# Banded attention: the next pair's query projection by group 3, eight parts of the pair beyond at the border; the dilated branch's log counts in seven steps

## What is computed

```python
def token_mixer(x, w_in, b_forget, sinks, w_branch, w_gate, b_gate, w_out):
    (aq, ak, av, bq, bk, bv, cq, ck, cv, ciq, cik, ciw, dq, dk, dv, df) = jnp.split(x @ w_in, offsets, axis=-1)
    o_a, _, _ = banded_attention(heads(aq, A_HEADS), heads(ak, A_KV_HEADS), heads(av, A_KV_HEADS),
                                 slopes_a, A_WINDOW - 1, 1, sinks)          # window 128, 8 heads on 2 kv heads
    o_b = dilated_attention(heads(bq, B_HEADS), heads(bk, B_HEADS), heads(bv, B_HEADS), slopes_b)
    o_c = dsa_attention(...)
    o_d = forgetting_attention(...)
    proj = jnp.einsum('bsnk,nkd->bsnd', branches, w_branch)
    gates = jax.nn.sigmoid(x @ w_gate + b_gate)
    return jnp.sum(gates * proj, axis=2) @ w_out
```

## Time and profile before

| | us |
|---|---|
| median of 3 runs | 2135.15 (2134.28 to 2136.54) |
| profiled execution, its time | 2136.81 |
| profiled execution, its span | 2135.0 |
| PE busy | 2073.9 |
| DVE busy | 1558.0 |
| ScalarE (ACT) busy | 973.4 |
| GpSimd (POOL) busy | 934.7 |
| mean granted clock of TensorE | 0.991 |

### The profile page before, as it was taken

One profiled execution on the slowest core, in us unless ns is written; L12 is line 12 of the kernel. 1 busy time (PEld: TensorE's weight loads), 2 busy tenths in 40 slices (PEclk: granted clock), 3 DMA queues, 4 the chain that ended last, 5 costly groups with the idle time before them and its releaser, 6 DMA issues.

```text
span 2135.0 us, 28861 instructions
## 1 busy us (share of the span) xinstructions
PE 2073.9 (97%) x10350; PEld 1729.5 (81%) x10350; DVE 1558.0 (73%) x2596; ACT 973.4 (46%) x1752; POOL 934.7 (44%) x732
## 2 busy tenths in 40 slices
PE   8799999999999999999999999999999999999998
PEld 6578887888887888888887888878788888888887
DVE  5669888767687666698775766667877777775668
ACT  4443333655633565615743665432433333334541
POOL 5367762333322332322332333534765555555751
PEclk9999999999999999999999999999999999999999
DMA  4123332110042111041031000341566565558862
GB/s 129 41 86 117 104 111 78 21 31 27 14 148 60 50 41 38 22 167 30 21 105 44 11 21 21 119 157 49 159 188 202 182 196 172 158 196 306 276 208 94
DMA packets 197374, 224.27 MB, mean 105 GB/s; under 512 B 25704, under 2 KB 149608, under 8 KB 197232
## 3 DMA queue, kind: packets, MB, share of 16 engines
q1 hardware_dynamic: 194320, 212.43, 31.8%
q10 hardware_dynamic: 2912, 10.00, 1.3%
HBM read 164.17 MB, written 58.23 MB: 104 GB/s over the span
## 4 chain that ended last, share of the span: by engine, by line
PE 80%; DVE 11%; ACT 3%; issue 3%; POOL 2%; DMA 1%; ACTq 0%; DVEq 0%
PE pair L1315 13%; PE pair L894 13%; PE pair L1181 7%; PE obank L1315 5%; PE pair L878 5%; PE pair L1344 5%; PE obank L988 4%; PE chunk L967 4%; PE pair L939 3%; PE chunk L1344 3%; PE obank L1181 3%; PE pair L1274 3%; PE pair L940 3%; PE obank L1344 2%; DVE o_top L2327 2%
## 5 line engine op out<-in xcount | busy, mean ns | idle before, releaser
L2116 POOL TENSOR_TENSOR w_lo<-w_raw,w_hi 128x1024 fp32r<-128x1024 f32 x64 | 158.6, 2479 | 320.7 <-ACT w_hi L1608 320.5
L2517 DVE TENSOR_TENSOR pt_lo<-chunk,pt_hi 128x512 fp32r<-128x512 f32 (+1 forms) x272 | 173.7, 639 | 86.3 <-ACT pt_hi L1631 82.5
L1631 ACT ACTIVATE pt_hi<-chunk 128x512 fp32r<-128x512 f32 (+1 forms) x272 | 150.8, 555 | 171.3 <-PE chunk L967 169.9
L2164 POOL TENSOR_SCALAR prob<-prob,att 128x256 f32<-128x256 f32 (+4 forms) x172 | 117.9, 696 | 237.6 <-DVE att L2453 237.6
L894 PE MATMUL pair<-act_hi,w_hi 128*128 128x512 f32 x432 | 187.5, 434 | 1.1 <-DVE heads L2458 0.9
L894 PE MATMUL pair<-act_hi,w_lo 128*128 128x512 f32 x432 | 170.8, 395 | 0.0
L894 PE MATMUL pair<-act_lo,w_hi 128*128 128x512 f32 x432 | 170.2, 394 | 0.0
L2327 DVE TENSOR_SCALAR_CACHE_REDUCE o_top<-score,stat 128x384 uint8<-128x384 f32 (+1 forms) x186 | 166.6, 941 | 0.4
L988 PE MATMUL obank<-pt_hi,heads 128*128 128x256 f32 (+1 forms) x568 | 148.8, 286 | 1.9 <-DVE o_t L2525 1.2
L1727 ACT ACTIVATE prob<-prob,att 128x256 f32<-128x256 f32 (+4 forms) x172 | 120.5, 701 | 47.7 <-DVE att L2441 46.2
L988 PE MATMUL obank<-pt_lo,heads 128*128 128x256 f32 (+1 forms) x568 | 139.2, 281 | 0.0
(11 more groups left out here) (492 smaller groups left out, 5963.1 us busy)
## 6 DMA issues: line engine op xcount, KB each, us to landing
down_sums<-dn_sums SPq DMA_DIRECT2D x40, 512.0 KB, 6.3
w_raw<-in_w_in SPq DMA_DIRECT2D x37, 512.0 KB, 3.8
gates<-o_t SPq DMA_DIRECT2D x22, 512.0 KB, 2.9
up_raw<-in_w_up SPq DMA_DIRECT2D x22, 512.0 KB, 4.8
gate_raw<-in_w_ffn_gate SPq DMA_DIRECT2D x22, 512.0 KB, 6.0
hidden<-gelu_s SPq DMA_DIRECT2D x22, 512.0 KB, 3.4
dn_raw<-down_sums SPq DMA_DIRECT2D x44, 256.0 KB, 3.8
h_in<-down_sums SPq DMA_DIRECT2D x44, 256.0 KB, 4.7
```

Of the source, the lines that this page charges most:

```text
L2116: nc.gpsimd.tensor_tensor(split_into(1, g), w_raw[:, g % 2, 0:kt * cols], split_into(0, g).bitcast(F32), ALU.subtract).then_inc(lo_ready, 1)
L2517: nc.vector.tensor_tensor(pt_lo[:, n % PT_SLOTS, 0:m], t[:, 0:m], pt_hi[:, n % PT_SLOTS, 0:m].bitcast(F32), ALU.subtract).then_inc(chunk_f ...
```

## The change

`BESIDE[A]` puts all parts for the next pair in groups 0 to 3 (before: up to group 6) and eight of the pair beyond in groups 7 to 9 (before: four in groups 8 and 9); `AHEAD[A]` goes from 4 to 8, so eight parts stand before pair 0's loop, now run through `beside_v`'s branch of the loop, `fill(4)` and `fill(4)`. `BESIDE_LAST[A]` is unchanged, its first eight of sixteen places now count for its own turn. In pair 0, 1 and 2 the copy "q0" h 0 stands after group 2 instead of 3. `ln_counts` counts in seven steps instead of thirteen (a floor of the distance as integer, the low bits shifted into a float, compared with zero and added in one step); the five steps of the logarithm and the two biases stay. Five steps instead of eleven run before B's query copies.

```diff
--- before.py
+++ after.py
@@ -191,8 +191,8 @@
               (10, 2), (11, 1), (11, 1), (12, 2), (12, 2), (13, 0), (13, 2), (15, 2), (15, 2), (16, 0),
               (16, 2), (16, 2), (18, 0), (18, 2), (19, 0), (19, 1), (19, 2), (20, 0), (20, 2), (21, 0),
               (21, 1), (21, 2), (21, 2), (21, 2)),
-          A: ((0, 1), (0, 2), (0, 2), (1, 0), (1, 2), (2, 1), (2, 2), (3, 2), (4, 2), (4, 2),
-              (5, 0), (6, 1), (8, 1), (9, 2), (9, 2), (9, 2)),
+          A: ((0, 1), (0, 2), (0, 2), (1, 0), (1, 2), (2, 1), (2, 2), (3, 1),
+              (7, 1), (7, 2), (8, 0), (8, 1), (8, 2), (9, 0), (9, 1), (9, 2)),
           D: ((0, 2), (0, 2), (1, 0), (1, 2), (1, 2), (2, 2), (2, 2), (3, 1), (3, 2), (3, 2),
               (4, 2), (5, 0), (5, 0), (5, 1), (6, 1), (7, 0), (7, 2), (7, 2), (8, 1), (8, 2),
               (9, 2), (10, 0), (10, 2), (10, 2), (11, 0), (11, 1), (11, 2), (12, 0), (12, 2), (12, 2),
@@ -219,7 +219,7 @@
             ((0, 2), (0, 2), (1, 2), (3, 0), (3, 1), (3, 1), (5, 2), (6, 2), (8, 2), (9, 2),
              (9, 2), (11, 0), (11, 0), (11, 1), (13, 0), (13, 2), (15, 0), (16, 2), (17, 1),
              (17, 2), (18, 1), (19, 0), (21, 2), (21, 2)))
-AHEAD = {A: 4}
+AHEAD = {A: 8}
 
 EARLY_GATES = {NKT - 3: 4, NKT - 2: 5, NKT - 1: 7}
 FIRST_C = 2
@@ -240,7 +240,7 @@
         return [(what, h) for at, what, h in gates + queries if at == g]
     if pr == PAIRS - 1:
         return ()
-    at = {A: ((3, "q0", 0), (5, "q0", 1), (6, "q1", None))}.get(
+    at = {A: ((2, "q0", 0), (5, "q0", 1), (6, "q1", None))}.get(
         br, ((3, "k0", 0), (6, "k0", 1), (10, "q0", 0), (14, "q", 1), (15, "q1", 0), (16, "k1", 0), (17, "k1", 1),
              (18, "v", 0), (21, "v", 1)))
     return [(what, h) for c, what, h in at if c == g]
@@ -1018,11 +1018,9 @@
                     transposes(0, 0)
                     if pr == 0:
                         pe.wait_ge(*staged_all)
-                    fill(2)
+                    fill(AHEAD.get(br, 4) // 2)
                     pe.wait_ge(*staged_all)
-                    transpose_tokens(stage(br), lambda n: fill(2 * n))
-                elif br == A and pr == 0:
-                    fill(AHEAD[br] // 2)
+                    transpose_tokens(stage(br), lambda n: fill(AHEAD.get(br, 4) // 2 * n))
                 for g in range(len(stream) + 2):
                     j, c = stream[g] if g < len(stream) else (NGROUPS, 1)
                     fill_at(g, 0)
@@ -2387,23 +2385,15 @@
             def ln_counts():
 
                 count, tmp, di = mid[:, 0, :], mid[:, 1, :], mid[:, 2, :].bitcast(U32)
-                own(nc.vector.tensor_scalar(mid[:, 3, :], dist[:], 4096.0, None, ALU.min))
-                yield
-                own(nc.vector.tensor_copy(di, mid[:, 3, :]))
-                yield
                 own(nc.vector.tensor_scalar(count, dist[:], 128.0, None, ALU.is_le))
                 yield
-                for window, dil in ((512, 4), (2048, 16)):
-                    own(nc.vector.tensor_scalar(tmp.bitcast(U32), di, dil - 1, None, ALU.bitwise_and))
+
+                for last, dil in ((513.0, 4), (4095.0, 16)):
+                    own(nc.vector.tensor_scalar(di, dist[:], last, None, ALU.min))
                     yield
-                    own(nc.vector.tensor_copy(mid[:, 4, :], tmp.bitcast(U32)))
+                    own(nc.vector.tensor_scalar(di, di, dil - 1, 24, ALU.bitwise_and, ALU.logical_shift_left))
                     yield
-                    own(nc.vector.tensor_scalar(mid[:, 4, :], mid[:, 4, :], 0.0, None, ALU.is_equal))
-                    yield
-                    own(nc.vector.scalar_tensor_tensor(tmp, dist[:], float(window), mid[:, 4, :],
-                                                       ALU.is_le, ALU.mult))
-                    yield
-                    own(nc.vector.tensor_tensor(count, count, tmp, ALU.add))
+                    own(nc.vector.scalar_tensor_tensor(count, di.bitcast(F32), 0.0, count, ALU.is_equal, ALU.add))
                     yield
                 own(nc.vector.tensor_scalar(tmp, count, 0.0, HUGE, ALU.is_equal, ALU.mult))
                 yield
@@ -2752,7 +2742,7 @@
                 elif kind == "q":
                     if step == ("q", B, 0):
                         dve.wait_ge(gate_product, len(GATE_PRODUCTS))
-                        counted(11)
+                        counted(5)
                     topk_parts(TOPK_FIRST.get(step[:2], 0))
                     if step == ("q", D, 0):
 
```

## The result

The changed kernel takes 2157.74 us in the median (2157.09 to 2158.42, 4 runs), the one before 2135.14 (2134.28 to 2136.54): a ratio of 1.0105, interval 1.0088 to 1.0123, or 22.6 us more. The profiled execution took 2158.42 us with a span of 2156.6, against 2136.81 and 2135.0 before.

The account below looks back on a forecast made before the run. PE bounds the kernel, so changes win only where it waits; DVE's queue sets the border wait. Branch A 16.2 + 1.3 = +17.5, counts -1.2, sum +16.3 on the profiled 2136.81; by the median 2151 us, range 2141 to 2161.

Parts of the forecast that it names:

- likeliest case: Whole kernel: the forecast itself, 2147 to 2157 us, chance 0.55.
- case of a deeper clock loss: Rival: half clock also meets the merge and pair 0's longer start, another 5 to 9 us, 2157 to 2162; chance 0.10.
- cause b: Branch A's borders: PE waits 1.7 us each because DVE's own queue, not the projection, makes the query copies late.
- Part 1: Branch A's borders: parts moved from groups 3 to 6 stand behind DVE's last query copy, +3.7 us per border.
- Part 2: Branch A, group 3: first query copy ahead of the softmax step delays GpSimd's split and DVE, +0.8 us per border.
- Part 3: Ends of branch A: eight parts ahead of pair 0's loop, not four, +2.7 us; last pair 0, bounds -2.8 and 0.
- Part 4: TensorE's clock falls at all three borders of branch A, 2.3 us each, +7.0, less 5.7 already in before: +1.3.
- Part 5: Branch B's log counts: key copies start 1.2 us earlier, PE's wait of 2.45 shrinks to 1.2: -1.2 us.

Follow-up runs that it names:

- e12: Kernel before with its twelve parts of groups 0 to 6 all in groups 0 to 3, all else as before: ratio 1.0036, 2144.3 us.
- e4: As e2, with the later two query copies after groups 3 and 5 instead of 5 and 6: ratio 1.0083 to the kernel before.
- e7: Kernel before, old counts, with query copies after groups 4, 5, 5, weight split after group 4, parts spread anew: ratio 0.9970, 2135.0 us against 2141.2.
- e10: As e2, with matmuls repeated over their own result to keep PE busy through its waits in pairs 0 to 2: ratio 1.0080 to the kernel before.
- e5: Kernel before with only the first query copy moved from group 3 to group 2: ratio 1.0002.
- e6: As e2, with the first query copy back after group 3: ratio 1.0103 to the kernel before.
- e9: As e2, with the last pair's eight parts spread over its groups 0 to 8 (BESIDE_LAST[A]): ratio 1.0081 to the kernel before.
- e2: Kernel before with the change of branch A alone (tables, AHEAD 8, first query copy), log counts as before: ratio 1.0108.
- e11: Kernel before with the first matmul of group 4's values repeated nine times in pairs 0 to 2: ratio 0.9979.
- e1: Kernel before with the log counts in seven steps and nothing else: ratio 1.0003.

## Why the prediction held, and where it missed

It said 2151, in 2141 to 2161, and slower; measured were 2157.74. The likeliest case had reached to 2157, and the case of a deeper clock loss lay above it; the result lies just inside the second, and that is in part luck. Of the two places that this case named, the start of pair 0 kept the clock, and the merge with the last pair made 2.6 us, not 5 to 9. Of the 5.3 us by which the profiled executions differ more than forecast, 2.9 come from falls of the clock in which the change has no part: 1.3 before 100 us, and 1.6 in B, where before's trace alone kept it up.

- **The bound: DVE's queue sets the fence (cause b).** Right. Projecting earlier alone left the wait and made the fence later (e12), copying earlier shortened it (e4), and doing both with the parts in DVE's shadow won (e7).
- **Part 1, 3.7 us more behind the fence.** Right to about a tenth once the clock is taken out: 4.56 before, 8.3 in e10. It did not name DVE's own wait of 3.5 to 4.7 us there, but the price is the same stretch.
- **Part 2, fence 0.8 later.** The size is right (0.8, 1.1, 1.0), the reason only half. On the order of before the copy does what the step said: e5's fence is 0.7 to 1.0 later and its pairs with like clock 0.8 and 0.6 longer. But taking it back on the changed order (e6) brings the fence only 0.2 forward: there the moved parts hold it by themselves, which the step did not see.
- **Part 3, start +2.7, last pair 0.** The start is +2.75. The last pair was the step that failed: it took 1.9 more, not 0 to -2.8. Its eight parts all stand in groups 0 to 4, and behind them PE waits 1.8 and 1.3 us for GpSimd (0.6 before), the clock falls, and the merge begins at the lower level (+0.7). The prediction had a loss there only in a rival (0.10). e9, with these parts spread, gave 2.1 back against e2; how the 1.9 divides between the waits and the clock is not shown.
- **Part 4, the clock.** Falls at all three borders, as forecast (and a fourth, above). PE's idle time in pairs 0 to 2 is 4.5, 5.1 and 5.4 us, from 2.1, not 6 or 7. The price of the falls was set at 2.3 each, 7.0; e10 against e2 gives 6.1 for three. The price of those in before was put at 5.7; e11 gives 5.4. The rule of the Trainium skill (TensorE: Matmul & The Clock Gate, What's actually happening), that the array is throttled unless recent activity releases it, is borne out here: matmuls that compute nothing new kept the clock at 1.00 in e10 and e11. The trace of before alone had not decided it.
- **Part 5, the counts, -1.2.** Wrong in size: 0.56 by the wait. The step counted that one of 1.23 us leaves DVE's queue between the query and the key copies. It passed over the integer step (L2394), which comes to stand behind the query copies: it and the count step take the place of the comparison and the addition, so 0.55 is saved and not 1.23. What the other steps save ahead of the query copies was rightly put at nothing: it shows as DVE's idle bracket of 4.11 us at 351.96. The forecast also took for granted that the clock stays up in B as in the one trace; it falls there in the others, with either version, so this is no part of the difference.

Sum of the misses in the profiled executions (16.3 forecast, 21.6 measured): last pair 1.9, merge 0.7, branch B 2.25 (-1.2 forecast, +1.05 in this pair of traces, 1.6 of that the clock's), 1.3 of the clock's fall before 100 us, less 0.4 in pairs 0 to 2 and 0.4 in the rest of the kernel.

## What to carry to other kernels

When an engine waits for a copy, see first whether the copying engine had an idle bracket ahead of it: if not, finishing its input sooner wins nothing, and the copy has to move in that engine's own queue. Filler work is free only where the filled engine waits for another; taken out of such a place and put behind a fence it costs its full length, and the hole that it leaves can cost the clock as well. It can also starve the very engine that sets the fence, when that engine's next input stands behind it. Where one trace shows the clock up at a place that is close to losing it, do not price a change against that single trace.

## What was not expected of the hardware

- The clock falls at the same place of the same instructions in one execution and not in another: pair 0 of A 28.68 us in before, 25.70 in e1; pair 1 25.92 and 28.80. Behind the first scores of B before's trace kept 1.00, and the ten traces whose instructions are the same up to there did not.
- Nine repeated matmuls of 128x256 (1.31 us) in front of a wait of 1.25 us, at each of three borders, kept the clock at 1.00 there and made the kernel 0.21% faster.
- A DVE step on integers that takes 0.69 us alone (L2394) took 2.39 when GpSimd's split ran beside it: it ended 0.55 us after the split did. In before it was the next kind of step, between two tiles in SBUF, that took 2.11 for 1.22. Whichever of the two comes first behind the copies waits out the split.
